# Seven of eight experts sorted on chip by token count, weights addressed by registers; the three smallest with 64 slots

## The reference, cut to what matters

```
def swiglu(h, w_gate, w_up, w_down):
    a = jnp.einsum('bsd,df->bsf', h, w_gate)
    u = jnp.einsum('bsd,df->bsf', h, w_up)
    return jnp.einsum('bsf,fd->bsd', jax.nn.silu(a) * u, w_down)

def moe_swiglu(h, w_router, w_gate, w_up, w_down):      # 8 experts, each 1024 x 2816 (gate, up) and 2816 x 1024 (down)
    logits = jnp.einsum('bsd,de->bse', h.astype(F32), w_router.astype(F32))
    top_val, top_idx = lax.top_k(logits, TOP_K_EXPERTS)  # 2 experts for each token
    top_w = jax.nn.softmax(top_val, axis=-1)
    combine = jnp.sum(jax.nn.one_hot(top_idx, N_EXPERTS, dtype=F32) * top_w[..., None], axis=-2)
    out = jnp.zeros_like(h)
    for e in range(N_EXPERTS):
        out = out + combine[..., e:e + 1].astype(h.dtype) * swiglu(h, w_gate[e], w_up[e], w_down[e])
    return out
```

## Time and profile before

| | us |
|---|---|
| median of 3 runs | 2799.75 |
| lowest and highest run | 2794.57, 2801.67 |
| profiled execution, first to last instruction (its span) | 2796.6 |

### The profile page before, as it was taken

One profiled execution on the slowest core, in us unless ns is written; L12 is line 12 of the kernel. 1 busy time (PEld: TensorE's weight loads), 2 busy tenths in 40 slices (PEclk: granted clock), 3 DMA queues, 4 the chain that ended last, 5 costly groups with the idle time before them and its releaser, 6 DMA issues.

```text
span 2796.6 us, 47173 instructions
## 1 busy us (share of the span) xinstructions
PE 2707.4 (97%) x20168; PEld 1795.0 (64%) x20168; DVE 1076.6 (38%) x2449; ACT 426.6 (15%) x1164; POOL 172.6 (6%) x282
## 2 busy tenths in 40 slices
PE   8999899999999998999999999999989999999998
PEld 7875457677778744577876658765545644655455
DVE  4772242367567503324774543444421001001002
ACT  1110252001101103220101321112311100101010
POOL 3100100000000002000000100001000000000000
PEclk9999999999999999999999999999999999999999
DMA  7954323466657542224764424443269999999996
GB/s 234 340 202 166 106 91 121 139 238 222 214 182 256 181 143 98 90 92 165 258 209 128 140 106 166 156 154 109 76 261 373 395 396 402 401 392 395 401 399 274
DMA packets 305890, 620.02 MB, mean 222 GB/s; under 512 B 15180, under 2 KB 172016, under 8 KB 305552
## 3 DMA queue, kind: packets, MB, share of 16 engines
q1 hardware_dynamic: 287088, 550.80, 54.7%
q0 software_dynamic: 18592, 66.17, 6.8%
HBM read 607.87 MB, written 9.05 MB: 221 GB/s over the span
## 4 chain that ended last, share of the span: by engine, by line
PE 84%; issue 10%; DVE 3%; DMA 1%; ACT 1%; POOL 1%; DVEq 0%; SPq 0%; POOLq 0%; ACTq 0%
PE psum L1111 21%; PE psum L1222 15%; PE psum L1070 12%; PE psum L1261 7%; PE psum L1615 5%; PE psum L1032 5%; PE psum L1353 3%; PE psum L1526 2%; PE psum L1636 2%; PE psum L1056 1%; PE psum L1059 1%; PE psum L1741 1%; PE psum L1693 1%; PE psum L1135 1%; PE psum L1236 1%
## 5 line engine op out<-in xcount | busy, mean ns | idle before, releaser
L1222 PE MATMUL psum<-ring,xT 128*32 128x512 f32 (+3 forms) x5376 | 465.5, 503 | 1.6 <-ACT xT L2039 1.6
L1070 PE MATMUL psum<-ring,hid 128*128 128x512 f32 x880 | 386.7, 592 | 0.0
L1222 PEld LDWEIGHTS psum<-ring,xT 128*32 128x32 f32 x5376 | 204.4, 110 | 245.7 <-issue 224.5
L1070 PEld LDWEIGHTS psum<-ring,hid 128*128 128x128 f32 x880 | 164.8, 190 | 195.6 <-issue 195.6
L2949 DVE SCALAR_TENSOR_TENSOR proj<-proj,psum 128x256 f32<-128x256 f32 (+1 forms) x72 | 28.4, 394 | 587.1 <-ACT proj L2053 587.1
L1261 PE MATMUL psum<-ring,proj 128*32 128x256 f32 x4224 | 233.4, 379 | 0.8 <-ACT proj L2065 0.8
L1261 PEld LDWEIGHTS psum<-ring,proj 128*32 128x32 f32 x4224 | 169.7, 110 | 65.9 <-issue 8.7
L1032 PE MATMUL psum<-ring,xT 128*128 128x512 f32 (+1 forms) x480 | 200.6, 580 | 2.2 <-DVE xT L2302 1.4
L1111 PE MATMUL psum<-xT,ring 128*128 128x128 f32 x1600 | 195.0, 275 | 0.0
L1111 PEld LDWEIGHTS psum<-xT,ring 128*128 128x128 f32 x1600 | 187.1, 192 | 0.3
L1032 PEld LDWEIGHTS psum<-ring,xT 128*128 128x128 f32 x480 | 91.1, 191 | 109.8 <-issue 107.3
(11 more groups left out here) (433 smaller groups left out, 3142.7 us busy)
## 6 DMA issues: line engine op xcount, KB each, us to landing
ring<-in_ffn_w_gu SPq DMA_DIRECT2D x88, 1024.0 KB, 6.5
ring<-in_w_exp_down SPq DMA_DIRECT2D x88, 1024.0 KB, 9.1
ring<-in_w_exp_gate SPq DMA_DIRECT2D x128, 512.0 KB, 7.1
ring<-in_w_exp_up SPq DMA_DIRECT2D x128, 512.0 KB, 9.0
ring<-in_ffn_w_down SPq DMA_DIRECT2D x44, 1024.0 KB, 9.5
xn<-in_w_ada POOLq DMA_DIRECT2D x24, 1024.0 KB, 8.5
proj<-in_w_ada POOLq DMA_DIRECT2D x24, 1024.0 KB, 8.7
ring<-in_w_exp_gate SPq DMA_DIRECT2D x64, 384.0 KB, 6.0
```

The lines of the kernel that those rows point to most:

```text
L1070: ins = mm(banks[2 * b + h][:, :], hid[f][:, b * P:(b + 1) * P], rows[:, f, h * 512:(h + 1) * 512], start=first, stop=last, skip_group_che ...
L1222: ins = mm(o[:, :, o0:o1], xg[e % 2][:, k, 32 * g:32 * g + 32], w_[:, :, c0:c1], start=(k == 0 and n_ == 0), stop=(k == KT - 1), skip_grou ...
```

## The change

After the router, DVE counts the tokens of experts 1 to 7 and sorts these seven by count (`ranks`). Expert 0 stays first with 96 slots. Positions 1 to 7 of the program get the ranks 0, 4, 1, 5, 2, 3, 6 (0 is the fullest), so the three smallest stand at positions 2, 4 and 7. These three have 64 slots in two groups; the others keep 96 in three. DVE writes the numbers of the experts in their new order into `order_i`, and SP reads one of them before each position's first load and addresses the weights by that register. The three small ones are marked by adding 32 to their counts and ranks, so that more than 64 tokens in one of them starts the late passes just as more than 96 in another. For two groups `down` writes 512 columns into four quarters of one bank, and the results of the last position are scattered by four matmuls.

With the inputs of the reference (seed 0) the reference's own router gives experts 0 to 7 the counts 67, 73, 79, 33, 61, 69, 70, 60. The three smallest of experts 1 to 7 have 61, 60 and 33.

The diff, cut to its core:

```diff
+RANKS = (0, 4, 1, 5, 2, 3, 6)
+SMALL = 4
+GROUPS_OF = (GROUPS,) + tuple(GROUPS - 1 if r >= SMALL else GROUPS for r in RANKS)
+CAPS = tuple(32 * n for n in GROUPS_OF)
+RANKED = NEXP - 1
+SPARE = S + 32 - CAP
...
+ROWS_AT = tuple(sum(CAPS[:p]) for p in range(NEXP))
+SLOTS = sum(CAPS)
...
                 for n, (what, e, (i, m), _) in enumerate(st["order_of_units"]):
                     u = st["n0"]["units"] + n
-                    g, up, down = ffn_weights(st, e)
+                    if e > whose:
+                        if e == 1:
+                            sp.wait_ge(sm["most_ready"], 1)
+                        whose = e
+                        number = sp.value_load(order_i[0:1, e - 1:e], min_val=1, max_val=NEXP - 1)
+                        held[e] = tuple(A[name][0][ds(number, 1)].rearrange("a k n -> (a k) n")
+                                        for name in ("w_exp_gate_2", "w_exp_up_2", "w_exp_down_2"))
+                    g, up, down = held[e]
...
-                            nc.gpsimd.dma_start(xrow_e[(e + 1) % 2][0:CAP, :], token_rows[(e + 1) * CAP:(e + 2) * CAP, :])\
+                            n = CAPS[e + 1]
+                            nc.gpsimd.dma_start(xrow_e[(e + 1) % 2][0:n, :], token_rows[ROWS_AT[e + 1]:ROWS_AT[e + 1] + n, :])\
...
+                        if GROUPS_OF[e] < GROUPS:
+                            for h in range(2):
+                                nc.gpsimd.dma_start(to[0:64, h * 512:(h + 1) * 512], t[64 * h:64 * h + 64, 0:512])\
+                                    .then_inc(sm[f"results_out{e % 2}"], 16)
+                            continue
...
                 def scatter_last():
                     t = ye[(NEXP - 1) % 2]
-                    pe.wait_ge(sm["gath_evac"], 2 * NEXP + 2)
-                    pe.wait_ge(sm["ye_dve"], 2 * NEXP - 1)
-                    for b in range(NB):
-                        mm(banks[b][:, :], selT[0:CAP, b * P:(b + 1) * P], t[0:CAP, 0:512], start=True, stop=True)\
-                            .then_inc(sm["scat_ready"], 1)
+                    pe.wait_ge(sm["gath_evac"], 2 * NEXP + 1)
                     pe.wait_ge(sm["ye_dve"], 2 * NEXP)
-                    for b in range(NB):
-                        bank = banks[(2, 7)[b]]
-                        mm(bank[:, 0:256], selT[0:CAP, b * P:(b + 1) * P], t[0:CAP, 512:768], start=True, stop=True, skip_group_check=True)
-                        for g in range(GROUPS):
-                            ins = mm(bank[:, 256:512], selT_last[g][:, b * P:(b + 1) * P], t[CAP:P, 256 * g:256 * g + 256],
-                                     start=False, stop=(g == GROUPS - 1), skip_group_check=True)
-                        ins.then_inc(sm["scat_ready"], 1)
+                    for h in range(2):
+                        half = slice(64 * h, 64 * h + 64)
+                        for b in range(NB):
+                            mm(banks[((0, 1), (2, 7))[h][b]][:, :], selT[half, b * P:(b + 1) * P], t[half, 0:512], start=True, stop=True)\
+                                .then_inc(sm["scat_ready"], 1)
 
...
-                        for g in range(GROUPS):
+                        for g in range(groups):
...
+                            if GROUPS_OF[e] < GROUPS:
+                                for g in range(4):
+                                    ins = mm(banks[5][32 * g:32 * g + 32, :], tokens[:, 32 * (g % 2):32 * (g % 2) + 32],
+                                             wt[:, f, 512 * (g // 2):512 * (g // 2) + 512], start=first, stop=last, skip_group_check=True)
+                                continue
...
+                    def ranks():
+
+                        numbers = C("slots")[:, 1:NEXP]
+                        link(V.tensor_copy(tokens, banks[6][:, 0:NEXP]))
+                        link(V.scalar_tensor_tensor(key, tokens[:, 1:NEXP], float(NEXP), numbers, ALU.mult, ALU.subtract))
+                        link(V.tensor_tensor(table, key.unsqueeze(1).to_broadcast([P, *square]), key.unsqueeze(2).to_broadcast([P, *square]),
+                                             ALU.is_gt))
+                        link(V.tensor_reduce(order, table, AX_X, ALU.add))
+                        V.memset(extra[:, 0:1], 0.0)
+                        V.memset(row[:, 0:1], 0.0)
+                        link(V.tensor_scalar(extra[:, 1:NEXP], order, float(SMALL), 32.0, ALU.is_ge, ALU.mult))
+                        link(V.tensor_tensor(hot, order.unsqueeze(1).to_broadcast([P, *square]),
+                                             C("rank_of").unsqueeze(2).to_broadcast([P, *square]), ALU.is_equal))
+                        link(V.tensor_tensor(table, hot, numbers.unsqueeze(1).to_broadcast([P, *square]), ALU.mult))
+                        link(V.tensor_reduce(key, table, AX_X, ALU.add))
+                        V.tensor_copy(order_i[:, :], key).then_inc(sm["most_ready"], 1)
...
+                        if GROUPS_OF[e] < GROUPS:
+                            for at in (0, 256):
+                                V.tensor_tensor(ye[e % 2][:, at:at + 256], banks[5][:, at:at + 256], gate_halves[:, at:at + 256], ALU.mult)\
+                                    .then_inc(sm["ye_dve"], 1)
+                            return
...
-                    select(0)
+                    select_first()
+                    ranks()
                     shares()
-                    most_now = dve.value_load(most_i[0:1, 0:1], min_val=0, max_val=S)
```

More of the change, by code:

```diff
@@ L27, with hidden_groups, three_groups @@
 GROUPS = CAP // 32
+RANKS = (0, 4, 1, 5, 2, 3, 6)
[4 more added lines that the diff above has]
+SPARE = S + 32 - CAP
 CHUNKS = ((0, 256), (1024, 256), (2048, 192))
 LATE_PASSES = 2
-SLOTS = NEXP * CAP
-RESULTS = SLOTS - CAP
-TOKEN_ROWS = SLOTS + NEXP * (S - CAP)
+ROWS_AT = tuple(sum(CAPS[:p]) for p in range(NEXP))
+SLOTS = sum(CAPS)
+RESULTS = ROWS_AT[-1]
+TOKEN_ROWS = SLOTS + NEXP * SPARE
+def hidden_groups(e, i):
+    return 3 * sum(GROUPS_OF[:e]) + (i * GROUPS_OF[e] if i else 0)
+def three_groups(e, i):
+    return 3 * sum(n == GROUPS for n in GROUPS_OF[:e]) + i * (GROUPS_OF[e] == GROUPS)
 EPS = 1e-6
@@ L165 @@
 CONST_FIRST = 2 * P
-N_ZEROS = SLOTS // P + 1
+N_ZEROS = -(-SLOTS // P) + 1
 N_SMALL, N_LATE = 36, 5
@@ L434, in build @@
         most_i = sb("most_i", [P, 1], I32)
+        order_i = sb("order_i", [P, RANKED], I32)
+        last_rank = sb("last_rank", [P, 3, NB])
         router_gain = lamv[:, 0, 0:2, :].rearrange("p a d -> p (a d)").rearrange("p (k e) -> p k e", k=KT)
@@ L1267, in experts @@
                 for e in range(NEXP):
-                    gate_up(e, 0, lambda k: turn_last(k // 4) if e == NEXP - 1 and k in (2, 6) else None)
+                    gate_up(e, 0, lambda k: turn_last() if e == NEXP - 1 and k == 2 else None)
                     if e:
@@ L2045, in tanhs @@
                         w = CHUNKS[i][1]
-                        for g in range(GROUPS):
-                            if g < GROUPS - 1:
-                                act.wait_ge(sm[f"chunk_done{g}"], n + 1)
+                        for g in range(GROUPS_OF[e]):
+                            if g < GROUPS_OF[e] - 1:
+                                act.wait_ge(sm[f"chunk_done{g}"], (n if g == 0 else three_groups(e, i)) + 1)
                             else:
@@ L2896, in _ @@
                     link(V.tensor_copy(rank[:, :, :], psum[:, 4:6, 0:NEXP]))
+                    tokens = xn[:, 0, 0:NEXP]
+                    extra = xn[:, 0, NEXP:2 * NEXP]
+                    row = xn[:, 0, 2 * NEXP:3 * NEXP]
+                    away = xn[:, 0, 3 * NEXP:4 * NEXP]
+                    key = xn[:, 0, 32:32 + RANKED]
+                    order = xn[:, 0, 40:40 + RANKED]
+                    square = (RANKED, RANKED)
+                    table, hot = (xn[:, 0, n:n + RANKED ** 2].rearrange("p (a e) -> p a e", a=RANKED) for n in (64, 128))
@@ new lines, in _ @@
+                    last_hot = hot[:, RANKED - 1, :].unsqueeze(1).to_broadcast([P, NB, RANKED])
+                    two = xn[:, 0, 192:192 + 2 * RANKED].rearrange("p (b e) -> p b e", b=NB)
+                    def ranks():
[13 more added lines that the diff above has]
+                        V.tensor_copy(order_i[:, :], key).then_inc(sm["most_ready"], 1)
+                        link(V.tensor_tensor(table, hot.rearrange("p a e -> p e a"), C("row_of").unsqueeze(1).to_broadcast([P, *square]),
+                                             ALU.mult))
+                        link(V.tensor_reduce(row[:, 1:NEXP], table, AX_X, ALU.add))
+                        link(V.tensor_tensor(row, row, extra, ALU.subtract))
+                        link(V.tensor_tensor(away, C("spare_row"), row, ALU.subtract))
+                        link(V.tensor_tensor(tokens, tokens, extra, ALU.add))
+                        link(V.tensor_tensor(rank[:, :, :], rank[:, :, :], extra.unsqueeze(1).to_broadcast([P, NB, NEXP]), ALU.add))
@@ new lines, in select_last @@
+                    def select_last():
```

(12 more changed lines are left out.)

113 lines of the change are left out of this document (58 added, 55 removed).

## The result

The changed kernel takes 2774.26 us (median of 4 runs, 2770.64 to 2776.95), the kernel before 2799.69 (4 runs, 2794.57 to 2801.67). The ratio is 0.9909, with a 95% interval of 0.9895 to 0.9923: 25.4 us less, where 14.4 were forecast.

What follows compares the result with a forecast made beforehand. PE was taken to bound the expert stage, with DMA at 408 GB/s only 2.4 us per position below it. The terms -4.9 - 1.6 - 5.5 - 2.4 sum to -14.4 us: 2785.4 us, range 2775 to 2794.

Steps and rivals of the forecast that it cites:

- Term (1): End of the expert stage: one two-group unit of 1.7 us instead of 6.6 us left after the last landing, -4.9 us.
- Term (2): POOL's queue at positions 2, 4 and 7: fewer token rows, 0.66 MB less at 408 GB/s, -1.6 us, upper bound 2.2.
- Term (3): DMA's dips vanish with the ring empty: 1.1 us at each of positions 2, 3, 4, 5 and 7, -5.5 us, bounds 0 to 12.0.
- Term (4): Tail after PE's last down matmul: the scatter's four matmuls take 3.8 us and end earlier, -2.4 us, bounds 1.5 and 3.3.
- The costs taken at nothing: SP's register loads and unit instructions, DVE's 3.5 us of ranking, the longer last selection: all counted as 0 us.
- DMA faster than 408: Rival in the expert stage: DMA speeds up when asked for more, 2711 to 2775 us; chance 0.05.
- DMA slower with a full ring: Rival: each percent below 408 GB/s costs 4.4 us over five positions, a loss beyond 3.3%; chance 0.14.
- SP the bound: Rival: register addresses make each of a position's 59 DMAs cost over 1.5 us; at 2 us about 3000; chance 0.01.
- late passes: Rival: a marked expert has over 64 tokens, so two more passes over 276.8 MB add 1357 us; chance 0.01.
- The clock fell to its lower level: Rival: PE's clock stays at half through the three small positions, 30.4 us more at each, 2890; chance 0.04.
- DMA at 405 or more: Sign in the profile after: DMA at 405 GB/s or more in every window from position 2 to 5.
- Landings 16 to 18 us after the issue: Sign at the small positions: weight loads land 16 to 18 us after issue, against a median of 9.1 before.

Runs made afterwards that it cites:

- twice: The changed kernel with every result row of positions 0 to 6 stored twice on POOL's queue: 2775.99 us, ratio 0.9914 to the kernel before.
- thin_256: The kernel before with 6% fewer columns in every expert matmul and its ring of weights at byte 88064: 2773.98 us, ratio 0.9911.
- thin: The kernel before with narrower matmuls at all experts, so PE asks for 6% more weights per us: 2791.59 us, ratio 0.9973.
- last_only: The changed kernel with the small size at position 7 alone, positions 2 and 4 back at 96 slots: 2787.36 us, ratio 0.9953 to the kernel before.
- static: The changed kernel with SP's register load taken out and weights addressed by constants in the same order: 2771.17 us, ratio 0.9900 to the kernel before.
- at147: The changed kernel with small positions 1, 4 and 7 instead of 2, 4 and 7: 2769.20 us, ratio 0.9891 to the kernel before.
- all_small: The changed kernel with 64 slots at all of positions 1 to 7, tokens beyond them left out: 2759.05 us, ratio 0.9860 to the kernel before.

## Why the prediction was right in its mechanism and wrong in its size

**The bound** was read right: at a small position PE is relieved of a third of its matmuls and gets back a tenth of its time. Position 2 was to shorten by 8 to 10 us and did by 9.4, and there PE waits for landings. PE's own price was put too low, 59.9 us where it is busy for 67.0, which costs nothing beside a DMA that needs more. The stage's end is the last landing plus one unit.

**Term (1)**, one unit behind the last landing: -4.9 forecast, -4.7 measured.

**Term (2)**, POOL's rows by their bytes, -1.6: `twice` gives 3.0 us for the results of positions 1 to 6, 4 x 0.39 + 2 x 0.26 = 2.1 MB more, 1.4 us per MB, so 0.66 MB are about 1 us, an estimate from one execution of each kernel. Somewhat less than forecast, and below the bound.

**Term (3) failed.** Its step was: "Over 20 us it is 408 GB/s at share 1.03; nowhere in the stage do the rows show a plateau above that", taken as DMA's limit in both kernels. It was the limit of a ring that starts off a multiple of 256 bytes, and the diff moved the ring. As an estimate, the slack that DMA gives back to a position with 96 slots is then not 1.1 us but 89.4 - 86.4 = 3.0 (by `thin_256`), five times 15.0, and with term (2) -16.6; the landing moved by -17.0. That the count of five fits is in part luck. The rates say where the time was won: 414, 413 and 415 GB/s over positions 2 to 4, 405 over position 5, 396 over position 6 and 405 from there to the last landing, where before it was 396 to 399 and, in the last stretch, 390.

The other half of the proof is the changed kernel with the ring back off its place. There the last unit starts, at its landing, at 2769.06 (at byte 87840) and 2766.76 (87936):

```profile
2769.06 3.28 PE L1288 MATMUL psum<-ring,proj 128*32 128x512 f32 x16 [2.00 <-DMA ring<-in_w_exp_down]
...
2766.76 1.92 PE L1287 MATMUL psum<-ring,proj 128*32 128x512 f32 x16 [0.51 <-DMA ring<-in_w_exp_down]
```

Against 2774.5 that is -5.4 and -7.7, of which 1.2 and 1.5 us were won before position 2 began. From the start of position 2 to the last landing it is -4.2 and -6.2 (535.6 and 533.6 us for 539.8), where terms (2) and (3) together said -7.1. The forecast of 2785.4 is the time of the change without the move: 2786.9, 2786.0 and 2782.2 were measured at three such places. The windows of positions 2, 3 and 4 in the kernel with the ring at 87840 show how:

```profile
2233.44:2316.22 82.78, 67.18 (x741) 26.69 (x740) 5.77 (x15) 7.35 (x22) 1.59 (x3) 1.00 1.03 403
2316.22:2406.88 90.66, 87.66 (x1131) 44.78 (x1131) 7.84 (x21) 8.43 (x25) 1.58 (x3) 1.00 1.03 403
2406.88:2492.65 85.77, 68.22 (x742) 26.16 (x741) 5.78 (x15) 7.35 (x22) 1.60 (x3) 1.00 1.03 403
```

They read 403 GB/s where the earlier trace rows has 397, 1.5% more or some 1.3 us a position, near the 1.1 of term (3); over positions 5 and 6 it is 398. So without the move term (3) is about the right size for a position and holds at three positions instead of five. `thin`, at the same place, read 398 to 403 over its positions 2 to 6 and shortened them by next to nothing. Why it gained less is open.

**Term (4)**, the tail: -2.4 forecast, -3.0 measured, which comes near for the wrong reason. Four matmuls of 512 columns on 64 rows took 2.00 us (timeline above, 2760.44), not 3.8, so by their time the two that read the upper half of the rows ran beside the two that read the lower. The scatter's end came 4.2 us nearer to PE's last down matmul, and by my own rows the bound for two halves at once should have been 4.3 and not 3.3. But I had let one addition of DVE, 0.75 us, stand behind the scatter. Now all four follow within 2.92 us, and the last ends 2.05 us behind the scatter instead of 0.78: 1.3 us are given back.

**The costs taken at nothing** were nothing or near it: `last_only` and `static` leave 0 to 3 us for ordering and registers together. An issue of SP's weight loads takes 0.33 and 0.38 us in the changed kernel and 0.33 and 0.43 with constants. Position 0 took 84.8 us in both kernels.

**The rivals.** DMA faster than 408 had 0.05 and is what happened, by a mechanism that I hadn't named: not "when asked for more" (`thin` asked and got 409). The ceiling of 435 GB/s in the Trainium skill (DMA: Bandwidth & Descriptors, Specifications) would have given about 2750, an estimate; 422 is the most that a window of 10 us shows here. DMA slower with a full ring: no, 419 GB/s in the window 2440 to 2450, where PE waited for every unit and all other slots were on their way. SP the bound, late passes: no sign. The clock fell to its lower level for about a unit in two places of the stage (below) and was 1.00 over positions 2 and 3; it didn't settle there.

**The signs that I had named.** DMA at 405 or more: yes over whole positions, 405 to 415, with 418 and more in stretches without POOL's rows, and a rate above 408 should have been a sign of its own. Landings 16 to 18 us after the issue: 10 to 15 in the medians of position 2, up to 17.6 beside POOL's rows. Gaps of 0.8 us: 0.53 in a steady stretch, because a unit of PE is 1.92 us, not 1.73, and landings are some 2.5 us apart (2744.51, 2747.00, 2749.46 in the timeline above). Large positions 88 to 91: 89.2 to 91.9, so one of them, position 5, lies above. Scatter 3.8 us: 2.0.

## What to carry to other kernels

A plateau of DMA is a limit of this program with these addresses, not of the chip: before it goes into a sum, look in the diff for all that moves a tile (a table of constants that gets shorter, a new tile ahead of a ring), and work out the buffer's start modulo 256 bytes before and after. And test "is it demand or capacity?" by thinning the consumer by some per cent: one run told it here. When two bounds lie within 1 or 2% of each other, relieving one of them gives little until the other is moved too, and moving the other alone gives next to nothing: here 11 us and 3 us each alone, 25 together. When the last step of a chain gets shorter, look at what the engine behind it still has to do.

## What the runs showed of the hardware

- DMA writing rows of 4096 bytes into SBUF, in stretches without POOL's rows: 418 to 422 GB/s into a ring that starts at byte 87808 or 88064 of the partition (0 modulo 256), 407 to 410 at 87840, 87872 and 87936 (32, 64 and 128 modulo 256), packets of 159 against 161 to 164 ns in the median; rows of 3072 bytes 121 against 124 to 125. Other remainders, places off a multiple of 32 bytes, and what part of the chip it is, were not tried.
- Float32 matmuls on two halves of the rows run side by side, by their time: four of 512 columns in 2.00 us, where two on 96 rows took 1.95.
- PE ran slower after some of its longer waits. In the changed kernel the unit that follows a wait of 3.09 us took 3.47 us instead of 1.92, with a granted clock of 0.66 over the 5 us around it (the lower of 1.2 and 2.4 GHz for a part of them), and the clock was 0.66 once more behind a wait of 2.17 us. Behind the first unit PE soon waited for a landing again (1.24 us, at 2714.47), behind the second it did not. At the end of the stage nothing covers it: in the kernel with the ring at 87840 the last unit, after a wait of 2.00 us, took 3.28 (its row is above), and in `at147`, after 2.05 us, 3.42. But after 1.92 us in `last_only` the last unit took 1.92, and after 2.10 us in `all_small` one did too, so the length of the wait alone doesn't decide it, and what does stays open.

```profile
2704.74 1.92 PE L1252 MATMUL psum<-ring,xT 128*32 128x512 f32 x16 [0.90 <-DMA ring<-in_w_exp_up]
2709.76 3.47 PE L1252 MATMUL psum<-ring,xT 128*32 128x512 f32 x16 [3.09 <-DMA ring<-in_w_exp_up]
...
2704.00:2709.00 5.00, 1.92 (x16) 0.42 (x16) 0.00 (x0) 0.00 (x0) 0.23 (x1) 1.00 1.03 417
2709.00:2714.00 5.00, 3.47 (x16) 0.59 (x16) 0.00 (x0) 0.00 (x0) 0.00 (x0) 0.66 1.03 420
```
